# x transposed a quarter at a time without its norm's factor, and the factor multiplied onto the outputs

## The reference

```python
def rms_norm(x, w):
    y = x32 * lax.rsqrt(jnp.mean(x32 * x32, axis=-1, keepdims=True) + EPS)
    return (y * w).astype(x.dtype)

for l in range(2):                       # first block
    h = rms_norm(x, norm_w[l]);  p = h @ w_in[l]
    # attention (128-wide window), convolution module, gated delta rule, each times silu(gate)
    x = x + concatenate([oa, ob, oc]) @ w_out[l]
for l in range(2):                       # second block: l = 0 pool mixer, l = 1 gated linear recurrence
    h = rmsnorm(x, g_pre[l]);  u, z = split(h @ w_in_2[l])
    y = mixer(u) * silu(z)
    x = x + rmsnorm(y @ w_out_2[l], g_post[l])
    e = sigmoid(rmsnorm(x, g_ple_in[l]) @ w_ple_gate[l]) * (p[l] @ w_ple[l])
    x = x + rmsnorm(e, g_ple_out[l])
```

## Time and profile before

| | us |
|---|---|
| median of 3 runs | 2733.72 (2732.63 to 2734.61) |
| profiled execution | 2733.27 |
| its span, first to last instruction | 2731.5 |
| PE busy | 2571.6 (94%) |
| DVE busy | 1651.6 (60%) |
| ACT busy | 1256.4 (46%) |
| mean granted clock of PE | 0.972 of full speed |

### The profile page before, as it was taken

How to read it: one execution, slowest core, us unless ns; L and a number is a source line. 1 busy time by engine, 2 the same in 40 slices (tenths; PEclk the granted TensorE clock), 3 DMA queues, 4 the chain that set the end, 5 groups by cost and what they waited for, 6 DMA issues and landing times.

```text
span 2731.5 us, 39690 instructions
## 1 busy us (share of the span) xinstructions
PE 2571.6 (94%) x17372; PEld 2362.0 (86%) x17372; DVE 1651.6 (60%) x1790; ACT 1256.4 (46%) x1349; POOL 0.2 (0%) x4
## 2 busy tenths in 40 slices
PE   6998999899998998999999999989799999998977
PEld 6997988679998887789989999868699999997766
DVE  4579756654788647555645556555646657556654
ACT  5444125544561245444444334355546565565453
POOL 0000000000000000000000000000000000000000
PEclk9999989999999989999999999999899999999999
DMA  6453223344442223545555555554354545544533
GB/s 225 157 184 108 93 78 111 144 172 176 171 155 78 93 85 109 196 168 180 181 194 182 186 190 180 193 204 144 121 183 170 185 174 181 185 170 155 202 121 123
DMA packets 62621, 430.61 MB, mean 158 GB/s; under 512 B 6896, under 2 KB 7024, under 8 KB 12400
## 3 DMA queue, kind: packets, MB, share of 16 engines
q1 hardware_dynamic: 60496, 414.97, 42.7%
q10 hardware_dynamic: 1952, 13.11, 1.2%
HBM read 421.76 MB, written 6.29 MB: 157 GB/s over the span
## 4 chain that ended last, share of the span: by engine, by line
PE 73%; DVE 13%; ACT 8%; issue 6%; DMA 0%; ACTq 0%; DVEq 0%; SPq 0%
PE PS L385 73%; ACT Q L822 4%; DVE WL L1376 3%; ACT WH L836 2%; DVE Q L1341 2%; DVE Q L1345 2%; DVE QA L1345 2%; DVE X L1345 1%; ACT L822 0%; ACT QA L822 0%; DVE HL L1345 0%; PE PS L654 0%; DVE Q L1352 0%; ACT HH L822 0%; DVE Y L1341 0%
## 5 line engine op out<-in xcount | busy, mean ns | idle before, releaser
L1376 DVE TENSOR_TENSOR WL<-W,WH 128x2048 fp32r<-128x2048 f32 (+2 forms) x388 | 860.3, 2225 | 708.2 <-ACT WH L836 708.2
L836 ACT ACTIVATE WH<-W 128x2048 fp32r<-128x2048 f32 (+2 forms) x388 | 717.0, 1857 | 596.8 <-PE PS L385 522.4
L385 PE MATMUL PS<-HH,WL 128*128 128x256 f32 x3392 | 563.0, 286 | 18.7 <-ACT QA L822 11.7
L385 PE MATMUL PS<-HL,WH 128*128 128x256 f32 x3392 | 557.0, 284 | 0.0
L385 PE MATMUL PS<-HH,WH 128*128 128x256 f32 x3392 | 556.7, 284 | 0.0
L385 PEld LDWEIGHTS PS<-HH,WL 128*128 128x128 f32 x3392 | 473.7, 193 | 23.7 <-issue 16.7
L385 PEld LDWEIGHTS PS<-HL,WH 128*128 128x128 f32 x3392 | 472.8, 193 | 0.0
L385 PEld LDWEIGHTS PS<-HH,WH 128*128 128x128 f32 x3392 | 472.4, 192 | 0.0
L385 PE MATMUL PS<-WL,HH 128*128 128x512 f32 (+2 forms) x768 | 230.9, 382 | 11.4 <-DVE HL L1341 11.4
L385 PE MATMUL PS<-WH,HL 128*128 128x512 f32 (+2 forms) x768 | 224.9, 374 | 0.0
L385 PE MATMUL PS<-WH,HH 128*128 128x512 f32 (+2 forms) x768 | 224.0, 373 | 0.0
(11 more groups left out here) (128 smaller groups left out, 2060.2 us busy)
## 6 DMA issues: line engine op xcount, KB each, us to landing
W<-in_wall SPq DMA_DIRECT2D x378, 1024.0 KB, 4.8
W<-in_wall SPq DMA_DIRECT2D x16, 512.0 KB, 3.5
W<-in_wall SPq DMA_DIRECT2D x8, 536.0 KB, 3.3
xsave<-X ACTq DMA_DIRECT2D x2, 2048.0 KB, 9.4
X<-xsave ACTq DMA_DIRECT2D x2, 2048.0 KB, 10.3
X<-in_x SPq DMA_DIRECT2D x4, 512.0 KB, 7.3
Q<-in_g_post ACTq DMA_DIRECT2D x2, 1024.0 KB, 4.7
Q<-in_g_ple_out ACTq DMA_DIRECT2D x2, 1024.0 KB, 8.0
```

The lines of the kernel that those rows point to most:

```text
L385: return e.matmul(o, l, r, start=start, stop=stop, skip_group_check=True)
L836: e.activation(WH[:, s % NSPL, 0:m], W[:, c % NRAW, 0:m], ACT.Copy).then_inc(*up("hi", c))
L1376: e.tensor_tensor(WL[:, c % NRAW, 0:m], W[:, c % NRAW, 0:m], WH[:, s % NSPL, 0:m].bitcast(F32), ALU.subtract).then_inc(*up("lo", c))
```

## The change

- **Transposition.** `norm` is gone. `turn(n, i)` transposes quarter i of X with the plain identity (`e.transpose`), 16 pieces. ACT and DVE evict as before, with the gain and without the factor (`upper`, `lower`).
- **Where it stands.** For n = 1, 2 quarters 0 to 2 are turned between the chunks of the last two output groups of the block before, into a spare tile XT first, and copied to HH and HL as these come free (`entry`); the last output group reads its chunks in the order soon, late. For n = 3, 5 the quarters are turned between the small groups of the post stage. What is left is turned inside the first group of the projection (`opening`).
- **The factor.** DVE forms DIAG as before, later; at the end of the opening group PE multiplies a matrix of ones by it and DVE copies the result to RBT (the factor of each position on all partitions). `scaled` is now the eviction of every such projection group: DVE multiplies PSUM by RBT. Gates and first taps are done by ACT from SBUF afterwards, as generators. Where positions are on the partitions, ACT's eviction takes the factor as its scale.
- **Side work.** Many `rest` counts change. The delta net's counts on PE become 29 + 11 + 4 + 3 + 4 + 1 + 4 + 25 + 2 + 16 + 1 = 100.
- **The recurrent layer's end.** Chain 6 does its product earlier; chain 7 runs beside the first half of the last output part and is finished before the second half.
- **Loads.** At the start the order is x0, x1, weights 0, x2, x3. Layer 0 doesn't save X and reads it back from the input. The post norm's gains come in quarters. In `post` DVE updates X before the ticks.

```diff
-        for part, gs in ((late, (0, 1)), (soon, (0, 1)), (late + soon, (2,)), (late + soon, (3,))):
+        for part, gs in ((late, (0, 1)), (soon, (0, 1)), (late + soon, (2,)), (soon + late, (3,))):
...
-            def norm(n):
...
+            def turn(n, i, *ready):
+                w.wait_ge(*to(*ready))
+                for k in (4 * i, 4 * i + 2):
+                    b = side(("norm", n, k), ("norm_a", n, "xt", k + 1) if n in (1, 2) and i < 3 else
+                             ("norm_v", n, "hl", k + 1))
                     for j in range(2):
                         for t in range(2):
                             c = 128 * (k + j)
-                            i = mm(b[:, 256 * j + 128 * t:256 * j + 128 * t + 128], X[:, t, c:c + 128], DIAG[:, t, :],
+                            o = e.transpose(b[:, 256 * j + 128 * t:256 * j + 128 * t + 128], X[:, t, c:c + 128], ident)
...
+            def opening(n, *steps, mode="cm"):
+                g = Group(from_h, lambda kt: [hl_of(n, kt)], 512, mode, 16)
+                for k in range(4):
+                    g.feed()
+                    if k < len(steps):
+                        turn(n, *steps[k])
+                if mode == "cm":
+                    b = side(("norm", n, "rb"), ("norm_v", n, "rb"))
+                    w.wait_ge(*to("norm_v", n, "diag"))
...
+                    mm(b[:, 0:256], ones, SM[:, 704:960]).then_inc(*up("norm_p", n, "rb"))
...
             def block1(l):
-                proj(l, 512)
+                if l:
+                    opening(1, (3, "ev_v", 19))
+                else:
+                    turn(0, 0, "x0", 0)
+                    turn(0, 1, "x1", 0)
+                    opening(0, (2, "x2", 0), (3, "x3", 0))
...
+                gc = mk()
+                gc.feed()
+                turn(n, 0, "ev_v", g16)
+                gc.feed()
+                turn(n, 1, "ev_v", g16 + 1)
+                gc.all()
+                gd = mk()
+                for k in SOON:
+                    gd.feed()
+                    if k == 0:
+                        turn(n, 2, "ev_v", g16 + 2)
...
-                proj(4, 512)
+                for i in range(2):
+                    turn(4, i, "x_v", "end", 0, i)
+                opening(4, *((i, "x_v", "end", 0, i) for i in (2, 3)))
...
+                    if i:
+                        turn(n, i - 1, "x_v", "mid", l, i - 1)
+                opening(n, (3, "x_v", "mid", l, 3), mode="tm")
...
+            def scaled(dst, g, nb=2):
+                for b in range(nb):
+                    tt(dst(b), pair(bank(g, b)), rb(2), ALU.mult, *(("ev_v", g) if b == nb - 1 else ()))
...
-                    yield from rest(28 if n == 6 else 12 if n == 7 else 4)
+                    yield from rest(16 if n == 6 else 4 if n == 7 else 5)
...
-                z_group[7] = group(4)
-                finish(ch)
+                scaled(lambda b: ZT[:, 4 + 2 * b:6 + 2 * b, :], group(4))
+                here["last"] = ch
                 out_part(1, 3, halves=2)
```

More of the change, by code:

```diff
@@ L491, in delta_net @@
             def delta_net(l):
[L492 removed]
+                yield from rest(21 + 8)
                 sq = sc(0, 3072)
@@ L866, in rstd, with skip, turned @@
                 act(o, o, ACT.Exp, "norm_a", "rstd", sid, scale=-0.5, bias=0.0)
-            def norm(gname, l, n):
-                off = AT[gname] + 16 * l
+            def skip(n):
+                for _ in range(n):
+                    tick()
+                here["g"] += 1
+                return here["g"] - 1
+            gain = {0: AT["norm_w"], 1: AT["norm_w"] + 16, 2: AT["g_pre_2"], 3: AT["g_ple_in_2"],
+                    4: AT["g_pre_2"] + 16, 5: AT["g_ple_in_2"] + 16}
+            def turned(n, k, dst, *name):
+                w.wait_ge(*to("norm_p", n, k))
+                for j in range(2):
+                    act(dst[:, k + j, :], sbank("norm", n, k)[:, 256 * j:256 * j + 256], ACT.Copy,
+                        "norm_a", n, *name, k + j, scale=TB[:, gain[n] + k + j:gain[n] + k + j + 1])
@@ L870, in norm, with upper @@
+            def upper(n, i):
                 if n:
                     w.wait_ge(*to("chunk", H_END[n]))
-                for k in range(0, 16, 2):
-                    w.wait_ge(*to("norm_p", n, k))
-                    for j in range(2):
-                        act(HH[:, k + j, :], sbank("norm", n, k)[:, 256 * j:256 * j + 256], ACT.Copy,
-                            "norm_a", n, "hh", k + j, scale=TB[:, off + k + j:off + k + j + 1])
-            def taps(l, i, n):
-                yield from rest(3 * n - 1)
+                for k in (4 * i, 4 * i + 2):
+                    turned(n, k, HH, "hh")
@@ new lines, in gate, with taps @@
+            def gate(v, g, *sig):
+                yield
+                w.wait_ge(*to("ev_v", g))
+                act(v, v, ACT.Silu, *sig)
+                yield
+            def taps(l, i, n, g):
+                yield
+                if l:
+                    w.wait_ge(*to("saved", l))
+                w.wait_ge(*to("ev_v", g))
+                for m in range(4 * i, 4 * i + n):
+                    wk = AT["c_conv_w"] + 72 * l + 54 + m
+                    act(CT[:, m, :], RAW[:, m, 3:259], ACT.Copy,
+                        *(("dn_a", l, "ct", i) if m == 4 * i + n - 1 else ()), scale=TB[:, wk:wk + 1])
+                yield from rest(3 * n + 6)
@@ L1144, in pool_layer @@
                     for i in range(2):
-                        gi = group(4)
-                        if g:
-                            w.wait_ge(*to("y_v", "pool", g - 1, 1))
-                        for b in range(2):
-                            act(ZT[:, 4 * i + 2 * b:4 * i + 2 * b + 2, :], pair(bank(gi, b)), ACT.Silu,
-                                *(("ev_a", gi) if b else ()))
+                        here["gate"] = begin(gate(ZT[:, 4 * i:4 * i + 4, :], skip(4), "u_a", "z", g, i))
                     if g > 0:
@@ L1163, in pool_layer @@
                         load_u(g + 1)
-                w.wait_ge(*to("y_v", "pool", 3, 1))
-                load_gains(0)
+                here["last"] = None
                 out_part(0, 3)
@@ new lines, in opening @@
+                for _ in range(2 if n == 4 else 3):
+                    tick()
+                w.wait_ge(*to("norm_p", n, "rb"))
+                copy(RBT[:, :], sbank("norm", n, "rb")[:, 0:256], "norm_v", n, "rb")
+                here["g"] += 1
+                w.wait_ge(*to("chunk", here["c"] - 1))
+                return here["g"] - 1
+            def scaled(dst, g, nb=2):
+                for b in range(nb):
+                    tt(dst(b), pair(bank(g, b)), rb(2), ALU.mult, *(("ev_v", g) if b == nb - 1 else ()))
@@ L1898, in post @@
                 total(3 + 4 * l)
-                for i in range(4):
-                    tick(again=i in (0, 2))
-                    here["g"] += 1
                 w.wait_ge(*to("norm_a", "rstd", 3 + 4 * l))
@@ L1907, in post @@
                             *(("x_v", "mid", l, i) if t else ()))
+                for i in range(4):
+                    tick(again=i in (0, 2))
+                    if i:
+                        lower(n, i - 1)
+                here["g"] += 4
+                lower(n, 3)
+                for _ in range(2):
+                    tick()
                 total(4 + 4 * l)
-                norm("g_ple_in_2", l, n, 4 + 4 * l)
                 w.wait_ge(*to("gple", l))
                 for i in range(4):
-                    g = group(4)
+                    g = group(4 if i else 2)
                     cs = slice(512 * i, 512 * i + 512)
```

527 lines of the change are left out of this document (310 added, 217 removed).

## The result

| | before | after |
|---|---|---|
| median of the runs, us | 2734.16 (2732.63 to 2735.08) | 2637.43 (2636.04 to 2639.04) |
| ratio, 95% interval | | 0.9647 (0.963 to 0.9664) |
| profiled execution: span, us | 2731.5 | 2636.4 |

The account below looks back on a forecast made before the run. PE's work plus its gaps, chiefly 67.7 us waiting on DVE's SM, was taken to bound the kernel. Gains of 8.5 + 7.7 + 14.0 + 14.5 + 6.9 + 8.0 + 13.3 + 10 = 82.9 gave 2650 us, range 2632 to 2680.

Parts of the forecast that it names:

- the mixer blocks: Both mixer layers: keys' 5.43 wait mostly goes, convolution's 3.19 goes; 10 us gained in all, from 10 lost to 22 gained.
- the start: Kernel start: first projection matmul at about 19.5 instead of 32.53 us; 8.0 us gained, 3 to 13.
- PE's gaps at the six norms: Ahead of each transposition of x, PE waits for DVE's SM: 67.7 us in six waits.
- A turn's price: Transposing a quarter of x, taken as 16 transposes: 1.75 us at full clock, 3.6 at low; all 64 cost 7.0.
- norms 1, 2, 3 and 5: Norms between blocks (1, 2) and inside post stages (3, 5): gains of 8.5, 7.7, 14.0 and 14.5 us.
- norm 4: Norm into the last layer: two quarters at low clock, HL 0 ready by then; 6.9 us gained.
- rival 1: Clock drops at the transposes of x: 2686 us, or 2723 with the transposes themselves low; chance 0.04.
- The tail of the delta net: Mixer blocks: last output product and norm run uncovered, with waits for v and ACT's square; 3.4 us lost a layer.
- Rival 2: Mixer blocks lose 10 us instead of gaining 10, DVE the bound and the tail bare: 2670 us; chance 0.14.
- Evictions elsewhere at nothing: Pool and recurrent layers: 32 groups' factor evictions move from ACT to DVE, 2 x 0.69 us each, at 0 cost.
- the layer's end: Recurrent layer's end: 7.28 wait falls to 1.5, 4.12 wait goes, 3.4 for the clock; 13.3 us gained.
- Rivals 3 and 4: 3: DVE becomes the bound, 2743 us, chance 0.04. 4: factor late at norm 4's opening and start, 2658, inside forecast's 0.78.

Follow-up runs that it names:

- kernel 2: Changed kernel, but in the two posts the four turns wait for the factor again, behind the small groups; median 2667.0 us against 2637.4.
- kernel 1: Changed kernel with each quarter of x transposed by eight ordinary fp32 products with the identity instead of eight transposes; median 2658.3 us against 2637.4.
- kernel 7: Changed kernel with the delta net's step counts cut by five on three engines, so it ends inside its 96 covering steps; median 2629.0 us against 2637.4.
- kernel 4: Two versions of the changed kernel with VectorE's factor evictions doubled: first in the mixer blocks only, 2651.3 us; second in pool and recurrent layers only, 2650.9; against 2637.4.
- experiment 5: Changed kernel with only the z groups' evictions (14) doubled on VectorE in the recurrent layer; median 2638.1 us against 2637.4.
- kernel 8: Changed kernel with the last recurrence finished ahead of the whole last output part again, not beside its first half; median 2642.5 us against 2637.4.
- kernel 9: Changed kernel with the rotary tables' VectorE operations moved behind the first group's eviction and ScalarE's sine behind the next; median 2636.6 us against 2637.4.

## Why the prediction was right, and where it was not

**The sum is nearer than its terms.** Norms (+17.7), recurrent layer (+4.5) and pool layer (+0.2) gave 22.4 us more than forecast, the mixer blocks (-9.2) and the start (-1.0) 10.2 less. That they cancel to 12.2 is luck.

**PE's gaps at the six norms set the time: right.** The waits on SM are gone, and kernel 2 loses 13.2 us for each norm in which only the wait and the order are restored. The prediction's first reading was a little off: it has the clock at 0.9 or more in every slice, and the row has three slices with an 8.

**A turn's price: wrong by a factor of two, the largest error.** I took a quarter of x as 16 transposes, from the 64 records in a norm of the earlier trace rows. It is 8, and the list of the change has the same slip ("16 pieces"); a norm before was 32 matmuls, not 64. An fp32 product leaves two records in the trace and a transpose one: x384 before, x192 after, x384 again in kernel 1. The 12 transposes of the earlier trace rows had been read rightly as 12; the mistake was to carry the product's count over. So a norm costs 3.5 us of turns and not 7.0. That is the whole excess of norms 1, 2, 3 and 5. In norm 4, where two quarters were reckoned at the low clock, the price alone gives 5.3 (two turns at 3.7 together in place of 7.2, two at 0.87 in place of 1.75), and the wait of 1.73 for the low half, which I had ready, takes nearly all of the difference back. The five norms gave 69.3 against 51.6.

**The clock at the turns: rival 1 is out.** The stretch 593:595 around a turn, and 1899.9:1903.6 around the first two of norm 4:

```profile
593.00:595.00 2.00, 2.00 (x20) 2.00 (x19) 1.08 (x1) 0.95 (x2) 0.00 (x0) 1.00 0.18 49
1899.90:1903.60 3.70, 3.68 (x16) 3.27 (x16) 3.56 (x5) 2.28 (x5) 0.00 (x0) 0.50 0.00 0
1905.30:1910.00 4.70, 4.68 (x39) 4.70 (x40) 4.19 (x10) 1.78 (x1) 0.00 (x0) 1.00 0.00 0
```

Between products a turn runs at 1.00, and behind a wait of 6.55 us at 0.50, as the products of kernel 1 do in that place (20 records in 4.64 us from 1920.69). The third row is stronger: between 1893.4 and 1905.3 PE did nothing but these 16 transposes and two waits, and the next product starts at 1.00. So transposes alone brought the clock up here; in some other profiles of the same code, kernel 7's for one, it was still low at that product (1.20 us). The Trainium skill, "TensorE: Matmul & The Clock Gate", section on the PE-mode transpose, has the full clock not engage for transposes. The trace does not agree. The same section of the Trainium skill gives about 275 ns for one tile of bf16 in a kernel's context. The trace agrees for fp32: one record of a turn lasts 270 ns at the least and 273 in the median. But eight of them overlap, and 0.79 us to the next product is 0.1 us each, so the duration of one is not its price.

**The mixer blocks: wrong by 9.2 us.** The keys' wait went from 5.43 to 4.74 and not to nothing. I had put VectorE's added evictions at 0.2 us of the sum beside a VectorE that was already busy 21.6 of 23 us; kernel 4 shows that over the two blocks half of every added us is PE's, with 3.3 us more at this wait. The delta net's first updates wait 2.88 where it was 1.52, and PE waits a new 1.61 at 452.50, ahead of the attention's transposes; neither was in the sum. The tail of the delta net was foreseen in kind (waits for v and for ScalarE's square), but I left out the clock behind them: 0.88 + 2.10, and 5.35 us for products that took 2.74 before, are 5.6 a layer and not 3.4. Kernel 7 gives 8.4 back. The convolution's 3.19 went as said, and some 3.6 us a layer of smaller waits (1.29, 0.17, 1.09, 1.08) went that no term had. Rival 2 was thus right about its mechanism and about half right about its size.

**Evictions elsewhere at nothing: right in the pool layer, wrong in one place of the recurrent one, lucky in the rest.** I argued from the bank's slack. That held for the pool layer (kernel 4, 0.0 us). In the recurrent layer kernel 4's 10.9 us come at the gates' steps, 1.4 to 1.5 each but for the first; at most of them the bank's release stands in ScalarE's queue behind a result of VectorE (experiment 5). The change could afford its evictions there because it reordered the same queue: PE's waits at those steps fell, of which this is one before (0.59 at 2038.93 after):

```profile
2100.52 0.71 PE L385 MATMUL PS<-HH,WL 128*128 128x256 f32 x4 [1.48 <-ACT QA L822]
```

Five such waits and the small ones of 0.31 ahead of them were in no term of the sum; some 5 us. At the layer's end I was right in sum for wrong reasons. The 7.28 went whole and not to 1.5, but not through the overlap. The 4.12 went whole as said, and by the overlap: without it (kernel 8) 2.96 of it come back, 2.4 in the sum. But there is a new wait of 2.50 at 2476.02, where I had none. It ends with the eviction of the last z group (VectorE in the changed kernel):

```profile
2474.46 1.41 DVE L1456 TENSOR_TENSOR Q<-PS,RBT 128x512 f32<-128x512 f32 x2
```

ScalarE did that eviction before; now it stands in VectorE's queue behind the last recurrence, and the group that PE does meanwhile lasts 5.6 us (from 2467.89) in place of 11.1, as the output part is done in halves. In kernel 4 this wait grows to 3.96. So here an eviction moved to VectorE has a price, and the sum had it at nothing.

**The start: about right, by luck** (17.95 for 19.5; term 7.0 for 8.0). The turns' price was wrong here too: the two ahead of the first product take 3.9 us and not 7.2, the two inside the group 1.8 less, and the first product came 1.5 earlier. Against that came, instead of the two chunk delays reckoned at 1 us, one wait of 3.59 us and the clock behind it. It is the rotary tables', a thing that stands in VectorE's order and that I did not look at (kernel 9). **Norm 4: right but for the low half**, as said above. **The order of updates in the posts:** norm 3's first turn has no wait and norm 5's 1.50 us. No kernel puts the updates back by themselves, so their share of the gain isn't shown. **Rivals 3 and 4** did not come: PE's waits for WL are the two at the start, 12.1 us, and no opening ends with a wait for the factor.

## What to carry to other kernels

A factor that only scales can be multiplied onto the outputs, and the transposes then need just the data: here that was worth 13 us for each norm in which only this order was tested. Count an operation's work from the code before taking a price from records, since the same tile can leave one record or two. Before putting work on an engine "with room", read its busy share in the stretch, not on the page, and ask in which queue order its result stands: doubled evictions cost nothing in the pool layer and half their time in the mixer blocks; in the recurrent layer those of the first seven z groups cost nothing, and a step with doubled u evictions 1.4 us.

## What the runs showed of the hardware

An fp32 transpose of 128 x 128 on TensorE costs 0.10 to 0.11 us in a row of 8 to 20 at granted clock 1.00, though one record lasts 0.27 us; an fp32 product of the same tile with the identity costs twice that (1.95 against 1.03 us for eight) and leaves two records. Transposes ran at clock 1.00 between products, and 16 of them alone, at 0.50, were followed by a product at 1.00 in the changed kernel.

Identical code in mixer block 0 took 528.8 or 533.9 us in different executions. The first large difference comes behind equal waits (0.87 and 0.88 us), with another granted clock behind them (0.72 and 0.83 over 30 us). The executions of one kernel lay between 2.5 us apart (the first of kernel 4, which has the longest waits in these blocks) and 11.4 (kernel 1), so the runs don't show that fewer waits make it less. A difference of 5 us was safe only stage by stage in the traces.
